# Gate products one tile ahead in two merge stages of a hybrid layer

## What is computed

```python
branch = jnp.einsum('bsnc,ncd->bsnd', ys, w_branch)      # ys: three branches, 256 x 1024 each
gates = jax.nn.sigmoid(gate_logits.reshape(bsz, seq, N_BRANCH, D_MODEL))
merged = jnp.sum(gates * branch, axis=2)
```

## The kernel before, in words

| stage | chunks | what |
|---|---|---|
| g0 and b0 | 112 to 159 | gate and `w_branch` product of the first branch, 16 tiles |
| xg | 160 to 175 | gate of the attention branch, 8 tiles |
| g2 and b2 | 176 to 223 | gate and `w_branch` product of the third branch, 16 tiles |
| g1 | from 224 | gates of the second branch |

## Time and profile before

### The profile page before, as it was taken

One profiled execution on the slowest core, in us unless ns is written; L12 is line 12 of the kernel. 1 busy time (PEld: TensorE's weight loads), 2 busy tenths in 40 slices (PEclk: granted clock), 3 DMA queues, 4 the chain that ended last, 5 costly groups with the idle time before them and its releaser, 6 DMA issues.

```text
span 2062.0 us, 30943 instructions
## 1 busy us (share of the span) xinstructions
PE 2005.4 (97%) x12224; PEld 1749.3 (85%) x12224; DVE 1571.2 (76%) x2489; ACT 978.3 (47%) x1439; POOL 410.8 (20%) x293
## 2 busy tenths in 40 slices
PE   7899999999999999999999999999999999999997
PEld 6787888888878888888799987888888888888886
DVE  8766888888799986697899986777567657656765
ACT  5445444444444445557543346544344434434442
POOL 2400134333334320000287644000000000000000
PEclk9999999999999999999999999999999999999998
DMA  7554555444445455565456664555555555555553
GB/s 294 195 182 166 184 182 173 161 166 154 166 161 175 164 188 180 187 220 196 139 181 199 200 206 144 184 190 188 193 186 193 189 190 191 188 193 186 192 190 117
DMA packets 106704, 378.02 MB, mean 183 GB/s; under 512 B 11968, under 2 KB 15808, under 8 KB 106560
## 3 DMA queue, kind: packets, MB, share of 16 engines
q1 hardware_dynamic: 106560, 376.04, 54.2%
HBM read 373.01 MB, written 2.98 MB: 182 GB/s over the span
## 4 chain that ended last, share of the span: by engine, by line
PE 79%; DVE 14%; ACT 2%; issue 2%; DMA 1%; SPq 0%; DVEq 0%; ACTq 0%
PE bank L1777 44%; PE bank L1779 23%; DVE bank L1545 3%; DVE wl L1003 3%; PE bank L1767 1%; PE bank L1766 1%; PE bank L1768 1%; ACT wh L643 1%; PE bank L1782 1%; PE bank L1784 1%; PE bank L1783 1%; PE bank L1806 1%; DVE sq L1010 1%; DVE uT L1054 1%; DVE scr L1034 1%
## 5 line engine op out<-in xcount | busy, mean ns | idle before, releaser
L1003 DVE TENSOR_TENSOR wl<-raw,wh 128x1024 fp32r<-128x1024 f32 x593 | 739.3, 1250 | 348.0 <-ACT wh L643 346.3
L643 ACT ACTIVATE wh<-raw 128x1024 fp32r<-128x1024 f32 x680 | 712.2, 1055 | 536.6 <-PE bank L1779 395.1
L1777 PE MATMUL bank<-Hr,wh 128*128 128x512 f32 x2432 | 860.9, 398 | 8.4 <-DVE wl L1003 4.1
L1777 PE MATMUL bank<-Yr,wh 128*128 128x512 f32 x2176 | 767.1, 396 | 16.1 <-DVE wl L1003 12.3
L1779 PE MATMUL bank<-Hr,wl 128*128 128x256 f32 x2432 | 682.6, 281 | 0.0
L1779 PE MATMUL bank<-Yr,wl 128*128 128x256 f32 x2176 | 610.5, 281 | 0.0
L1777 PEld LDWEIGHTS bank<-Hr,wh 128*128 128x128 f32 x2432 | 457.9, 188 | 121.2 <-issue 7.1
L1777 PEld LDWEIGHTS bank<-Yr,wh 128*128 128x128 f32 x2176 | 408.9, 188 | 113.5 <-DVE wl L1003 11.3
L1779 PEld LDWEIGHTS bank<-Hr,wl 128*128 128x128 f32 x2432 | 461.2, 190 | 0.3
L1779 PEld LDWEIGHTS bank<-Yr,wl 128*128 128x128 f32 x2176 | 412.0, 189 | 0.2
L586 POOL TENSOR_TENSOR wl<-raw,wh 128x1024 fp32r<-128x1024 f32 x87 | 215.0, 2480 | 410.2 <-ACT wh L643 387.3
(11 more groups left out here) (321 smaller groups left out, 1759.9 us busy)
## 6 DMA issues: line engine op xcount, KB each, us to landing
raw<-in_w_up SPq DMA_DIRECT2D x128, 512.0 KB, 4.3
raw<-in_w_dn SPq DMA_DIRECT2D x128, 512.0 KB, 4.3
raw<-in_w_g SPq DMA_DIRECT2D x96, 512.0 KB, 3.2
raw<-in_w_p SPq DMA_DIRECT2D x80, 512.0 KB, 3.2
raw<-in_w_b SPq DMA_DIRECT2D x48, 512.0 KB, 3.2
raw<-in_w_out SPq DMA_DIRECT2D x32, 512.0 KB, 3.2
raw<-in_w_bx SPq DMA_DIRECT2D x16, 512.0 KB, 5.1
raw<-in_w_q SPq DMA_DIRECT2D x16, 512.0 KB, 3.5
```

Source lines behind the costliest of these rows:

```text
L643: e.activation(wh[:, c % WN, :], raw[:, c % RAW, :], ACT.Copy).then_inc(s_hi, 1)
L1003: e.tensor_tensor(wl[:, c % RAW, :], raw[:, c % RAW, :], wh[:, c % WN, :].bitcast(F32), ALU.subtract).then_inc(s_low_v, 1)
L1777: e.matmul(dst.rearrange("p (h t) -> p h t", h=2), lh, pair.both[:, :, k, :], start=first_part and kk == 0, stop=last_part and kk == 7, sk ...
```

## The change

In both merge stages the gate product of tile t+1 is put ahead of the `w_branch` product of tile t. The order is now g(0), g(1), b(0), g(2), b(1), ..., g(15), b(14), b(15). Nothing else is changed: the number of chunks, of instructions and of bytes is the same, and in the middle of a stage the pattern is still two chunks of a gate and one of `w_branch`. The chunk with which a product ends is another one:

| | before | after |
|---|---|---|
| end of g(t), counted from the first chunk of the stage | 3t + 2 | 2 for t = 0, else 3t + 1 |
| end of b(t) | 3t + 3 | 3t + 5, and 48 for t = 15 |

```diff
     for t in range(8):
         one("au", t, "W", "w_au", t, 2)
         one("ag", t, "W", "w_ag", t, 2)
+    one("g0", 0, "W", "w_g0", 0, 2)
     for t in range(16):
-        one("g0", t, "W", "w_g0", t, 2)
+        if t < 15:
+            one("g0", t + 1, "W", "w_g0", t + 1, 2)
         one("b0", t, "W", "w_b0", t, 1)
     for t in range(8):
         one("xg", t, "W", "w_xg", t, 2)
+    one("g2", 0, "W", "w_g2", 0, 2)
     for t in range(16):
-        one("g2", t, "W", "w_g2", t, 2)
+        if t < 15:
+            one("g2", t + 1, "W", "w_g2", t + 1, 2)
         one("b2", t, "W", "w_b2", t, 1)
```

## The result

The changed kernel takes 2070.63 us (median of 10 runs, 2068.84 to 2075.66), the kernel before, run beside it, 2065.27 us (10 runs). The ratio is 1.0026 with a 95% interval of 1.0018 to 1.0034, so it is slower, by some 5.4 us. Its profiled execution took 2068.84 us with a span of 2066.7 us.

What follows compares the result with a forecast made beforehand. PE was taken to bound the kernel (97% busy), alone in g0/b0, with DVE close behind in g2/b2. +6.3 - 1.4 = +4.9 us on the median 2066.3 gave 2071 us, with an 8-in-10 range of 2064 to 2078.

Steps and rivals of the forecast that it cites:

- both terms: +6.3 us added in stage g0/b0 by new waits, and -1.4 us removed in stage g2/b2.
- The four waits: In g0/b0, PE's score product waits for `pT` once per head: 2.3, 1.0, 1.7 and 1.35 us, sum 6.35.
- The 0.16 us for a slower `wl`: In g0/b0's first head, `wl` with POOL beside it takes 1.39 instead of 1.23 us, lengthening the wait.
- qT: In g0/b0, `qT` copies of i = 10 behind a tanh cost 0.6 us; copies of i = 11 give back 0.6.
- The first rival: New waits in heads 1 and 3 of g0/b0 also drop the clock, DVE later: +8.9 us, 2075 us; chance 0.36.
- The stage g2/b2: PE keeps only what the ACT and DVE chain gets shorter by up to chunk 225: -1.4 us.
- a gain of 3.8 us: In g2/b2, the 2.3 us wait at the first b2 product and the slow clock behind it go.
- one meeting point: At the recurrence's products before chunk 225, PE follows DVE (716.41, 716.56), so PE's earlier gains are lost there.
- 0.9 us of work: By iteration 222 in g2/b2, DVE has one b2 way out fewer (1.25 us), one gate's addition more (0.35).
- 0.4 us of idle time: DVE's idle time behind the gates' additions in g2/b2 falls from 8.8 to 8.4 us with the new ends.
- The second: g0/b0 costs only 2.4 us, PE keeps 4 or 5 of 5.5: -2.1, 2064 us; chance 0.14 with the third.
- the third: Attention in g0/b0 absorbs its later copies, only g2/b2 remains: -1.4, 2065 us; chance 0.14 together with the second.

Runs made afterwards that it cites:

- second profile: The changed kernel itself run and profiled once more, with no further edit; ratio 1.0024 to the kernel before.
- The kernel before with copies first: The kernel before, with ACT's attention copies (steps i = 4, 9, 10, 11) issued ahead of a product's way out in the same iteration; ratio 1.0001.
- the end spread out: The changed kernel with ACT's attention copies ahead of the way out, plus the first g1 product put between the last two b2 products; ratio to before 0.9987.
- only the first pair exchanged: The kernel before, with g2/b2 starting g(0), g(1), b(0), b(1) and the old order from g(2) on; ratio 0.9999.

## Why the prediction was right, point by point

The time, 2070.6 against 2071 us, came out, and so did the signs of both terms.

**The four waits.** The step that carried the sum was: ACT cannot make `pT` before the tanh, which cannot come before DVE's `wl` and addition. The runs show it: the waits are at line 1871 behind `pT`, one in each head, and they go when the copy is put ahead of the tanh, with the ends of the products left where they are. The path of the earlier trace rows, 2.33 us, is 2.32 in the first head. The start of its `wl` was also right: 367.85 us, and as chunk 112 starts 0.81 us earlier in this execution than in the one before, that is the predicted 368.66. The 0.16 us for a slower `wl` was a misreading: 1.39 us is the mean of a pair, and the `wl` that counts took 1.22. Head by head, the step grew by (second profile) 2.24, 1.61, 1.65 and 1.11 us, where 2.3, 1.0, 1.7 and 1.35 were forecast: 6.6 against 6.35 us. Head 2 was mis-sized, because a `wl` ahead of the one that matters took 1.72 us, POOL being at work for 0.6 us of it:

```profile
408.52 1.72 DVE L1007 TENSOR_TENSOR wl<-raw,wh 128x1024 fp32r<-128x1024 f32 x1
...
412.20 1.21 DVE L1007 TENSOR_TENSOR wl<-raw,wh 128x1024 fp32r<-128x1024 f32 x1
```

That is 0.5 us over the usual 1.22. It is no accident of one execution: the same `wl` took 1.73 us in the second profile and 1.72 us with only the first stage changed. In the trace before, the `wl` of that iteration took 1.23 us, and the forecast had no term for it. Why it is slow was not tested.

**qT.** The prediction took +0.6 us for the copies of i = 10 and -0.6 for those of i = 11. Measured in the second profile, the steps of 122, 134, 146 and 158 grew by 1.34 us and those of 123, 135 and 147 fell by 0.53. The net is +0.8 instead of 0: the copies of i = 10 cost more than twice the forecast. Chunk 157 got shorter by 0.40 us, which nothing in the prediction foresaw. The stage as a whole: +6.8 against +6.3 us.

**The clock.** The first rival wanted a lower clock behind the first and the third head, and a later DVE: +8.9. One piece of it came true in the first profile: the 1.5 us at chunk 117, from which the stage cost 8.3 us there. It isn't part of the change's price in the median: in two of the three profiles with this wait the clock stayed up. The Trainium skill's page TensorE: Matmul & The Clock Gate, Part 1, has the half clock as the default, which activity releases. The forecast read it so that each wait of this length would cost the clock again; one profile here agrees and two do not, so it was right not to take that for certain. The third head's wait, 1.4 us, was followed by no lower clock in either profile of the changed kernel.

**The stage g2/b2.** Forecast -1.4, measured -1.2 us in six profiles of five kernels (200.71 to 200.79 us against 201.94). That a gain of 3.8 us would shrink to this because DVE's chain has its own time was argued from one meeting point, before chunk 225. The kernel before with copies first shows the mechanism directly: 1.5 us sooner at chunk 180, and nothing of it left at 185. The other three profiles of this order are that of the attention one chunk early (-0.9), that with `wl` on POOL (+0.9) and that with the end spread out, in which the clock fell (+0.1).

What was not right is how the -1.4 was built, and that its size came out is in good part luck. It had DVE's path to its last product before chunk 225 shorter by 0.9 us of work and 0.4 us of idle time. DVE from the `wl` of iteration 177, 11.2 us behind the start of chunk 176 in both kernels, to the end of that product, before and after:

```profile
573.67:716.41 142.74, 140.76 (x850) 118.37 (x850) 132.63 (x201) 62.78 (x104) 54.71 (x56) 0.99 0.50 170
581.16:720.95 139.79, 135.73 (x828) 113.64 (x827) 130.73 (x198) 63.79 (x104) 54.23 (x54) 1.00 0.50 169
```

The path is shorter by 2.9 us: DVE works 1.90 us less and stands 1.05 us less. By the forecast's reasoning PE should have kept 3 us. It did not, because it no longer meets DVE there:

```profile
719.35 0.41 DVE L1038 TENSOR_TENSOR scr<-scr,bank 128x256 f32<-128x256 f32 x1
...
719.81 0.49 PE L1781 MATMUL bank<-Hr,wh 128*128 128x512 f32 x1 [0.21 <-DVE scr L1038]
...
720.28 0.67 DVE L1329 TENSOR_TENSOR wm<-bank,wcs 128x512 f32<-128x512 f32 x1
...
722.79 0.64 PE L1853 MATMUL bank<-turned_s,Cs 128*32 128x256 f32 x8
```

DVE's product ends at 720.95 us and PE comes for it only at 722.79. PE was held before, at the first g1 product, whose bank g(15) held: its addition ends at 719.76. In the kernels where PE comes there sooner it waits 1.1 us, and starts chunk 224 the same 1.2 us sooner than before the change. So in the changed kernel the time of g(15)'s way out decides the 1.2 us, and in the kernel with only the first pair exchanged it is the idle time behind g(1). Nothing in the runs ties the two; that they come to the same number looks like chance.

Nor was the wait of 1.9 us before chunk 205 named at its place. PE met DVE's chain there, where DVE has the whole way out of a b2 tile and then the two products of the recurrence:

```profile
659.34 0.41 DVE L1038 TENSOR_TENSOR scr<-scr,bank 128x256 f32<-128x256 f32 x1
659.77 0.52 DVE L1088 SCALAR_TENSOR_TENSOR scr<-scr,scr 128x256 f32<-128x256 f32 x1
...
660.32 0.83 DVE L1091 TENSOR_TENSOR Mf<-Mf,scr 128x256 f32<-128x256 f32 x1
...
661.08 0.68 DVE L1328 TENSOR_TENSOR wm<-bank,wcs 128x512 f32<-128x512 f32 x1
661.68 0.67 DVE L1329 TENSOR_TENSOR wm<-bank,wcs 128x512 f32<-128x512 f32 x1
...
662.50 0.64 PE L1853 MATMUL bank<-turned_s,Cs 128*32 128x256 f32 x8 [1.93 <-DVE wm L1329]
```

**The other rivals.** The second (small waits, most of the stall kept) and the third (the attention absorbs it) are both excluded by the four waits.

## What to carry to other kernels

When the order of products changes, look first at what is tied to their ends and what is tied to the loop's count: here a copy of 0.36 us got behind a back-and-forth of 2.3 us between two engines, and cost more than the removed stall gave. In an in-order queue, put the short operation for which the busiest engine waits ahead of one that itself waits for a third engine; with that, a change that lost 0.26% gained 0.12%. And before a stall is counted as a gain, find the next place where the same two engines meet, in the new order and not in the old one: here it moved by a chunk.

## What the runs showed of the hardware that I had not expected

Waits of equal length did not bring the clock down each time. After the 2.27 to 2.30 us at the first b2 product the granted clock fell in two of three profiles. After the 1.98 to 2.0 us of the first head it fell in one of three. After the 1.9 to 2.0 us before chunk 205 it fell in one of eight. The time lost was 1.5 to 1.7 us each time. What decides it is not in these traces.

PE's pace in an undisturbed stretch differs between profiles at a granted clock of 1.00. From chunk 224 to 252, where the order is the same in all kernels but the one with its end spread out, it took 81.9 us in four profiles (before, after twice, first pair) and 83.3 to 83.6 us in the seven others without `wl` on POOL, 2.77 against 2.83 us for nearly every chunk. It is as large as the gains that were looked for here, which is why these are read from stages between fixed chunks and not from spans. Both paces occur within g2/b2 in the six profiles that give 1.2 us there, and PE's waits for DVE take the difference up. Its cause stays open.

A `wl` on POOL can hold up an instruction of DVE beside it. Beside the ten on POOL from chunk 176 to 225, those of DVE that took long read both inputs from SBUF: 1.1 to 2.5 us instead of 0.4 to 0.5. Those that read a PSUM bank, at the same time, took their usual 0.4 and 0.7 us.
